# Thirteen low-part subtractions go from VectorE to GpSimd, and q and k are normalised ahead of the last convolution taps

## The reference, cut to what matters

```
xn = rmsnorm(x, norm1_g) * (1 + sc1) + sh1          # sc, sh, g: silu(c) @ ada_w + ada_b
q, k, v, ca, cg = split(xn @ w_in)                  # 8 heads x 64; 512 channels of convolution
q, k = rmsnorm(q, q_norm_g), rmsnorm(k, k_norm_g)   # per head
y_attn = softmax(q k^T / 8 + rel_bias, causal) @ v
a = causal_dwconv(ca * sigmoid(cg), 31 taps)
a = silu(group_norm(a, 8 groups))
x = x + g1 * (concat(y_attn, a) @ w_out)
xn2 = rmsnorm(x, norm2_g) * (1 + sc2) + sh2
u, g = split(causal_dwconv(xn2 @ w_up, 3 taps))     # 2 x 2816
x = x + g2 * ((silu(g) * u) @ w_down)
```

## Time and profile before

| | |
|---|---|
| median of 3 runs | 377.09 us (376.81 to 379.04) |
| the profiled execution | 377.13 us, its span 375.3 us |
| PE busy | 352.0 us (94%) |
| DVE busy | 267.4 us (71%), of it 108.2 us in 47 `w_lo` subtractions |
| ACT busy | 176.9 us (47%) |
| POOL busy | 23.9 us (6%) |
| chain that ended last | PE 80%, DVE 12%, ACT 3%, DMA 3% |

### The profile page before, as it was taken

One profiled execution on the slowest core, in us unless ns is written; L12 is line 12 of the kernel. 1 busy time (PEld: TensorE's weight loads), 2 busy tenths in 40 slices (PEclk: granted clock), 3 DMA queues, 4 the chain that ended last, 5 costly groups with the idle time before them and its releaser, 6 DMA issues.

```text
span 375.3 us, 6080 instructions
## 1 busy us (share of the span) xinstructions
PE 352.0 (94%) x2408; PEld 295.6 (79%) x2408; DVE 267.4 (71%) x486; ACT 176.9 (47%) x251; POOL 23.9 (6%) x67
## 2 busy tenths in 40 slices
PE   1999899999499989999999999999999999999995
PEld 1677788897245437777799899998989899999984
DVE  0393799999996558756888776768586667658665
ACT  3442833352102465837674553635544644636430
POOL 7421000000000200002300000000000000000000
PEclk9999999999889899999999999999999999999999
DMA  8999958798774496551074544654635545510003
GB/s 317 428 422 417 366 209 329 260 344 346 312 289 160 152 371 261 203 199 47 2 283 167 220 148 194 221 165 176 223 123 217 186 160 215 176 50 2 3 0 113
DMA packets 12653, 79.51 MB, mean 212 GB/s; under 512 B 1352, under 2 KB 2768, under 8 KB 3280
## 3 DMA queue, kind: packets, MB, share of 16 engines
q1 hardware_dynamic: 12416, 78.97, 55.2%
q10 hardware_dynamic: 144, 0.13, 0.1%
q0 software_dynamic: 64, 0.01, 0.0%
HBM read 78.05 MB, written 1.06 MB: 211 GB/s over the span
## 4 chain that ended last, share of the span: by engine, by line
PE 80%; DVE 12%; ACT 3%; DMA 3%; issue 1%; POOL 0%; SPq 0%; DVEq 0%; ACTq 0%; POOLq 0%
PE bank L853 22%; PE bank L854 21%; PE bank L855 21%; DVE bank L621 5%; PE bank L875 4%; DVE w_lo L543 2%; PE bank L898 2%; PE bank L1096 2%; PE bank L909 1%; DMA xt<-in_x_t 1%; DMA raw<-in_stream 1%; PE bank L1116 1%; PE bank L1106 1%; PE bank L1018 1%; ACT w_hi L336 1%
## 5 line engine op out<-in xcount | busy, mean ns | idle before, releaser
L853 PE MATMUL bank<-act_hi,w_hi 128*128 128x256 f32 x480 | 137.8, 287 | 2.7 <-DVE glu L630 1.1
L543 DVE TENSOR_TENSOR w_lo<-raw,w_hi 128x2048 fp32r<-128x2048 f32 x47 | 108.2, 2303 | 42.1 <-ACT w_hi L336 42.0
L854 PE MATMUL bank<-act_lo,w_hi 128*128 128x256 f32 x480 | 135.7, 283 | 0.0
L855 PE MATMUL bank<-act_hi,w_lo 128*128 128x256 f32 x480 | 135.6, 283 | 0.0
L853 PEld LDWEIGHTS bank<-act_hi,w_hi 128*128 128x128 f32 x480 | 91.8, 191 | 9.3 <-issue 4.0
L336 ACT ACTIVATE w_hi<-raw 128x2048 fp32r<-128x2048 f32 x47 | 89.7, 1908 | 15.1 <-DMA raw<-in_stream 14.1
L854 PEld LDWEIGHTS bank<-act_lo,w_hi 128*128 128x128 f32 x480 | 92.0, 192 | 0.4
L855 PEld LDWEIGHTS bank<-act_hi,w_lo 128*128 128x128 f32 x480 | 91.9, 191 | 0.0
L621 DVE SCALAR_TENSOR_TENSOR bank<-glu,cols,bank 128x256 f32<-128x256 f32 x116 | 46.2, 492 | 0.0
L503 ACT ACTIVATE bias<-bank,cols 128x256 f32<-128x256 f32 x44 | 22.3, 557 | 35.7 <-PE bank L855 35.7
L853 PE MATMUL bank<-w_hi,hid_hi 128*128 128x512 f32 x88 | 34.8, 396 | 0.0
(11 more groups left out here) (155 smaller groups left out, 337.4 us busy)
## 6 DMA issues: line engine op xcount, KB each, us to landing
raw<-in_stream SPq DMA_DIRECT2D x71, 1024.0 KB, 5.5
xt<-in_x_t SPq DMA_DIRECT2D x1, 1024.0 KB, 4.9
bias<-toeplitz_rows SPq DMA_DIRECT2D x1, 1024.0 KB, 10.5
xr<-in_x_rows SPq DMA_DIRECT2D x1, 1024.0 KB, 9.6
out<-xmod SPq DMA_DIRECT2D x3, 256.0 KB, 2.0
gates_b<-in_ada_b_gates SPq DMA_DIRECT2D x1, 256.0 KB, 8.5
cols<-in_cols SPq DMA_DIRECT2D x1, 185.0 KB, 2.4
out<-xmod SPq DMA_DIRECT2D x1, 128.0 KB, 1.8
```

The lines of the kernel that those rows point to most:

```text
L543: nc.vector.tensor_tensor(w_lo[:, m % PARTS, :], slot(*SPLIT[m]), w_hi[:, m % PARTS, :].bitcast(f32), ALU.subtract).then_inc(lo_done, 1)
L853: nc.tensor.matmul(o, sh, mh, start=first, stop=False)
L854: nc.tensor.matmul(o, sh, ml, start=False, stop=False)
L855: return nc.tensor.matmul(o, sl, mh, start=False, stop=last)
```

## The change

The low parts of the slots m = 3 to 15 (`POOL_LOW`) are subtracted on GpSimd, with a semaphore `lo_pool_done` of their own; all others stay on VectorE. GpSimd does m = 3 to 9 after its first five `act_lo`, m = 10 to 14 after the two squares of the group norm, and m = 15 after the two residual sums. PE and SP wait for the semaphore of the engine that makes the slot. `LOW_AT_HEAD` is gone. And VectorE takes only 6 taps, not all that are left, between `qk_rstd` and the first `qk_normalise`; the last 16 taps come after the fourth `qk_normalise`.

```diff
+POOL_LOW = list(range(3, SP_AT["up", 1] + 1))
+
+
+def lows_through(m):
+
+    on_pool = sum(p <= m for p in POOL_LOW)
+    return m + 1 - on_pool, on_pool
...
+        def low_done(eng, m):
+
+            by_dve, by_pool = lows_through(m)
+            if m in POOL_LOW:
+                eng.wait_ge(lo_pool_done, by_pool)
+            else:
+                eng.wait_ge(lo_done, by_dve)
...
-        LOW_AT_HEAD = {1: SP_AT["out", 0], 4: SP_AT["out", 1], 5: SP_AT["out", 2], 6: SP_AT["out", 3], 7: SP_AT["up", 0]}
...
-                        sp.wait_ge(lo_done, SP_AT[k0, i0] + 1)
+                        low_done(sp, SP_AT[k0, i0])
...
+            def split_lo(m):
+
+                pool.wait_ge(hi_done, m + 1)
+                arrived(pool, *SPLIT[m])
+                if m >= PARTS:
+                    pool.wait_ge(w_used, m - PARTS + 1)
+                nc.gpsimd.tensor_tensor(w_lo[:, m % PARTS, :], slot(*SPLIT[m]),
+                                        w_hi[:, m % PARTS, :].bitcast(f32), ALU.subtract).then_inc(lo_pool_done, 1)
...
-                if m >= len(SPLIT):
+                if m >= len(SPLIT) or m in POOL_LOW:
                     return
...
-            taps(len(TAPS))
+            taps(6)
             qk_normalise(0)
             qk_normalise(1)
...
             qk_normalise(2)
             qk_normalise(3)
+            taps(len(TAPS))
...
-                if h in LOW_AT_HEAD:
-                    split_lo(LOW_AT_HEAD[h])
...
-            split_lo(SP_AT["up", 1])
-
...
-                pe.wait_ge(lo_done, m + 1)
+                low_done(pe, m)
```

More of the change, by code:

```diff
@@ L171, in hymba_layer @@
         ada_used, w_used = sem("ada_used"), sem("w_used")
-        hi_done, lo_done = sem("hi_done"), sem("lo_done")
+        hi_done, lo_done, lo_pool_done = sem("hi_done"), sem("lo_done"), sem("lo_pool_done")
         silu_c_ready, xsq_ready, ssq_ready, rms_ready = (sem(s) for s in ("silu_c_ready", "xsq_ready", "ssq_ready", "rms_ready"))
@@ L305, in _ @@
                                         ALU.subtract).then_inc(xn_lo_pool, 1)
+            def split_lo(m):
[5 more added lines that the diff above has]
+                                        w_hi[:, m % PARTS, :].bitcast(f32), ALU.subtract).then_inc(lo_pool_done, 1)
+            for m in POOL_LOW:
+                if m <= SP_AT["v", 1]:
+                    split_lo(m)
             for g in range(2):
@@ L310, in _ @@
                                         conv[:, 2 * g:2 * g + 2, :], ALU.mult).then_inc(gn_sq, 1)
+            for m in POOL_LOW:
+                if SP_AT["v", 1] < m <= SP_AT["up", 0]:
+                    split_lo(m)
             pool.wait_ge(xr_ready, 16)
@@ L315, in _ @@
                 nc.gpsimd.tensor_tensor(xr[:, t, 0:512], xr[:, t, 0:512], tmp[:, 2 * t, :], ALU.add).then_inc(x2_left, 1)
+            split_lo(SP_AT["up", 1])
             for k in range(1, KT, 2):
```

## The result

The changed kernel takes 392.63 us (median of 4 runs, 389.47 to 395.9), the kernel before on the same chip 377.5 (376.81 to 379.04). The ratio is 1.034, 95% interval 1.028 to 1.040: slower; it is taken without the execution of 395.9 us, which ran in a slower state, so it is not the quotient of these medians. The profiled execution took 389.47 us, its span is 387.7 us, 12.4 more than before.

What follows compares the result with a forecast made beforehand. VectorE was taken as late from 45 to 102 us, PE as the bound from 122. Terms -4.2 + 2.9 + 4.5 + 4.5 + 4.0 = +11.7 on 377.13 gave 388.8 us, range 378 to 393.

Steps and rivals of the forecast that it cites:

- The front: Before the first head: seven subtractions leave VectorE, the wait for `qk_inv` goes, first turn at 117.9 for 122.08: -4.2 us.
- GpSimd's price: Every moved slot: GpSimd takes 4.5 us for one low part, harmless in the front.
- Holding for the whole instruction: Heads and second norm: VectorE's SBUF-to-SBUF operations stand still until GpSimd's instruction ends, each meeting costing up to 4.5 us.
- m = 11: Head 3: GpSimd's slot holds VectorE's division until 143.2, so PE turns the head late: +2.9 us.
- m = 15: Second norm: the slot behind GpSimd's second residual sum holds VectorE's own second sum until 180.7: +4.5 us.
- m = 10 and 14: In the heads: these slots meet no VectorE operation that could be held, so they cost nothing.
- m = 12 and 13: Around `mix_parts`: GpSimd's two slots delay the division of head 6 to 162.6, PE turns it at 162.8: +4.5 us.
- Rival 2: Slower by less: one or two meetings go VectorE's way, giving 383 to 384.6 us, or 379 with both; 20%.
- The clock: Half clock behind three new PE waits of 2.9 to 4.5 us, 1.3 us taken for each: +4 us.

Runs made afterwards that it cites:

- The heads and the norm alone: The kernel before with only m = 10 to 15 on GpSimd and the taps in the old order: 394.93 us, ratio 1.035.
- the best version: Against the kernel before: m = 3 to 9 on GpSimd, old tap order, 16 taps ahead of the `qk_stat` wait, eight idle transposes before the first turn: 369.13 us, 0.970.
- the quartered kernel: The changed kernel with each GpSimd low part made by four instructions of 512 columns instead of one of 2048: 387.15 us, ratio 1.017 against the kernel before.

## Why the prediction was right

The forecast was 388.8 us, the profiled execution took 389.47, the median 392.63, near the upper end of the range (393). The mechanism, that a slot on GpSimd holds VectorE to its end and PE then waits, came out as forecast. That the number is so close is in part luck: in the trace the four terms other than the clock make +5.9 us where +7.7 was forecast, and the clock makes +6.5 where +4.0 was. By its steps:

- **The front.** Scores at 110.9 forecast, 110.68 measured; first turn 117.9, measured 117.56. That the 16 taps would be late next is what PE's wait of 2.4 us for them shows. `qk_inv` starts at 93.97. (PE's waits there are 2.4 and 1.4 us, about the 4 forecast; the stretch that the prediction names, 111.8 to 117.9, is 6.1 us long and not 7.) But -4.2 was also taken as what the front is worth, with the clock behind the first turn at the price of before, and that is a mis-sized term: alone, the front is worth 1.7 us (ratio 0.9955), since the clock around and behind its first turn falls short of full speed by 6.9 us, where it did by 1.8. The heads and the norm alone cost 13.1, where their terms add up to 15.9. The two misses nearly cancel: -1.7 + 13.1 = 11.4, forecast 11.7 (the intervals of the two ratios are wide, 1.3 and 3.7 us to either side).
- **GpSimd's price** of 4.5 us for a slot: 4.57, and no slot of the front was late. The Trainium skill, GPSIMD Engine Reference, section 3.1, has 4497 ns for a two-input operation of this size; the trace agrees: its rows of one slot take 4.50 to 4.60 us.
- **Holding for the whole instruction**, which rows of 1.3 us had shown, holds at 4.5 us, and quarters of the instruction free VectorE after a quarter. That is also the rule of the Trainium skill (SBUF — State Buffer, "Who interferes with whom"), and the trace agrees, with 4.3 us for the residual sum.
- **m = 11**: +2.9 forecast, a wait of 2.72. **m = 15**: +4.5 forecast, 4.39. **m = 10 and 14**: nothing, and nothing measured.
- **m = 12 and 13**: +4.5 forecast by way of the division of head 6; measured 3.33 by another way. The forecast took the times of before, "since the stages shift as one", and here they didn't. From the turn of head 4 to `add_bias` of head 6 it is 5.0 us before and 6.6 after, with the half level from 147 to 151 between them, while ScalarE begins high part 12 at 5.3 us behind that turn in both. So m = 12 met the small `npeak` of head 6 ahead of `mix_parts`, and m = 13 came late enough to meet nothing. In the kernel with only the heads and the norm on GpSimd (6.0 us) both slots met `mix_parts`, neither a division, and PE waited 7.57. Rival 2 came true for m = 13, and took off only 1.2 us (3.3 for 4.5). The stage was right; the operation that was caught and the size were decided by tenths of a microsecond.
- **The clock** was the term that was mis-sized: +4.0 on the three waits and nothing net at the front. The span grew by 12.4; -4.5 at the first turn and waits of 2.7, 3.3 and 4.4 make +5.9; so 6.5 us are left. The clock is large enough for them: in 1 us windows after the first turn, with PE at work, it falls short of full speed by 9.8 us in all, where it did by 1.7 before. The forecast priced three stretches, one behind each wait; there are five, and the one from 147 to 151 follows no wait of its own. This term also varies between executions: 389.47 us at a mean granted clock of 0.967 and 393.87 at 0.951 for one kernel.

What I could not separate: how much each single wait contributes to the clock. Only the wait before the first turn was filled on its own, and only in the best version, not in the changed kernel; the 6.5 us are what is left of a sum, not a measurement.

The forecast was silent on something the experiments show: of the two halves of the change, the new order was a loss by itself, and the front without it is 1.6 to 2.1% faster than the kernel before. I had priced the 16 taps at the front (-4.2 in place of -7.4 us) but did not name the old order as the better one.

## What to carry to other kernels

A free engine is not free work: before moving an operation from VectorE to GpSimd, list what VectorE does in the same microseconds. In these traces an operation with two SBUF inputs (the residual sum, 5.00 us for 0.68), or a cast or scaling from SBUF to SBUF (`npeak`, 4.57 for 0.17), stood still until GpSimd's instruction ended, however small it was; the taps, with an input in PSUM, did not. So give GpSimd long instructions only where VectorE works out of PSUM, and short ones elsewhere. When a wait is removed, look at what is queued behind the next step on that engine, and put the work that nobody waits for into its idle time ahead of the chain, not behind it. And price a wait of PE with a half-clock stretch behind it, as a risk and not as a fixed sum: here a stretch fell 1.7 us or more short of full speed, and it did not come every time.

## What the runs showed of the hardware that I had not expected

- An operation of VectorE on 128 x 2 elements, 0.17 us when free, was held for 4.57 us, as long as the residual sum on 128 x 512 (5.00 for 0.68, so 4.3): what it was held for didn't depend on its size.
- Eight idle transposes (1.04 us) in a wait of PE of 0.93 us took 3.0 us off the whole kernel, and the mean granted clock is 0.995 to 1.00 with them and 0.986 to 0.991 without, in the same session. The wait is not enough to bring the half level, since one execution in nine without the transposes ran at 1.00 throughout.
- A stretch at the half level can come with PE at work all the time: at 147 to 151 in the changed kernel, where PE is busy from 140.0 on.
- When the two engines both have operations of the kinds that hold each other waiting, they alternate one by one, as in the quartered kernel (1.77 and 1.64 us for two operations of 0.68).
